# Hybrid attention block: value products in their own PSUM bank, scores in three single banks, sigmoid products on VectorE, and another place for the threshold search

## What is computed

```python
h = _rmsnorm(x, g_in)
proj = h @ w_in            # queries, keys, values, gate paths of A, B, C, and merge gates
y_a = _sliding_window_sink_attention(a_q, a_k, a_v, attn_sinks)
# B: per query, an indexer's scores pick 256 keys, and only these are attended to
score = jnp.einsum('bqhs,bqh->bqs', jax.nn.relu(logits), wb)
_, sel = lax.top_k(score, topk)
y_c = _memory_cross_attention(c_q, m_k, m_v)
ys = jnp.stack([y_a * jax.nn.silu(a_z), y_b * jax.nn.silu(b_z), y_c * jax.nn.silu(c_z)], axis=2)
u = jnp.einsum('bsnc,ncd->bsnd', ys, w_branch)
merged = jnp.sum(jax.nn.sigmoid(gates.reshape(b, s, N_BRANCH, D_MODEL)) * u, axis=2)
return x + merged @ w_out  # then a final RMSNorm
```

## Time and profile before

| what | us |
|---|---|
| median of 3 runs | 3220.39 |
| lowest and highest | 3218.98, 3224.93 |
| the profiled execution, its own time | 3227.78 |
| its span, from first to last instruction | 3225.8 |
| TensorE matmuls busy in it | 2703.2 |
| VectorE busy | 1658.9 |
| ScalarE busy | 1426.6 |
| GpSimd busy | 607.9 |
| mean granted TensorE clock | 0.926 of 2.4 GHz |

### The profile page before, as it was taken

How to read it: one execution, slowest core, us unless ns; L and a number is a source line. 1 busy time by engine, 2 the same in 40 slices (tenths; PEclk the granted TensorE clock), 3 DMA queues, 4 the chain that set the end, 5 groups by cost and what they waited for, 6 DMA issues and landing times.

```text
span 3225.8 us, 37577 instructions
## 1 busy us (share of the span) xinstructions
PE 2703.2 (84%) x13724; PEld 2257.2 (70%) x13724; DVE 1658.9 (51%) x3208; ACT 1426.6 (44%) x2598; POOL 607.9 (19%) x473
## 2 busy tenths in 40 slices
PE   5989896788898987988898987898889969667796
PEld 4777775666687876766787866786667758566685
DVE  4454544332553647323654657732386575666621
ACT  4454543342553624332753535543286455344521
POOL 4435262252111210111111210011101102000020
PEclk9999997989899999989999988998999989888998
DMA  5557283275353340254353340025433505100044
GB/s 167 188 165 254 89 271 91 83 251 169 131 169 119 124 138 1 98 177 134 120 168 119 119 136 7 1 78 185 136 131 123 162 21 192 52 1 1 1 136 158
DMA packets 169701, 392.28 MB, mean 122 GB/s; under 512 B 12848, under 2 KB 95792, under 8 KB 159536
## 3 DMA queue, kind: packets, MB, share of 16 engines
q1 hardware_dynamic: 169520, 389.89, 37.0%
HBM read 301.76 MB, written 88.08 MB: 121 GB/s over the span
## 4 chain that ended last, share of the span: by engine, by line
PE 54%; DVE 19%; ACT 10%; issue 8%; POOL 5%; DMA 3%; SPq 0%; ACTq 0%; DVEq 0%; POOLq 0%
PE PJ L684 39%; PE TR L572 6%; PE PJ L642 3%; DVE prob L1147 3%; DVE ptL L1185 3%; ACT prob L795 2%; ACT ptH L817 2%; POOL pairs L960 2%; ACT squared L774 1%; DVE ranks L1279 1%; DVE above L1226 1%; DMA xs<-in_x 1%; ACT prob L805 1%; DVE zs L1215 1%; PE SC L712 1%
## 5 line engine op out<-in xcount | busy, mean ns | idle before, releaser
L684 PE MATMUL PJ<-hH,pairs 128*128 128x512 f32 (+1 forms) x3584 | 1129.1, 391 | 12.2 <-POOL pairs L960 6.8
L684 PEld LDWEIGHTS PJ<-hH,pairs 128*128 128x128 f32 x3584 | 675.5, 190 | 155.8 <-POOL pairs L960 8.7
L684 PE MATMUL PJ<-hL,pairs 128*128 128x512 f32 (+2 forms) x1792 | 697.5, 389 | 0.0
L572 PE MATMUL TR<-identR,prob 128*128 128x128 f32 x1480 | 260.5, 303 | 206.5 <-ACT prob L795 156.1
L1185 DVE TENSOR_TENSOR ptL<-TR,ptH 128x512 fp32r<-128x512 f32 (+1 forms) x384 | 255.6, 669 | 266.0 <-ACT ptH L817 264.3
L684 PEld LDWEIGHTS PJ<-hL,pairs 128*128 128x128 f32 (+1 forms) x1792 | 340.0, 190 | 67.8
L1226 DVE TENSOR_SCALAR_CACHE_REDUCE above<-score,bits 128x256 uint8<-128x256 f32 (+10 forms) x280 | 348.1, 1243 | 54.3 <-POOL zs L996 45.1
L572 PEld LDWEIGHTS TR<-identR,prob 128*128 128x128 f32 x1480 | 192.0, 155 | 260.9 <-ACT prob L795 175.4
L828 ACT ACTIVATE signs<-score,bits 128x384 bf16<-128x384 f32 (+7 forms) x256 | 334.6, 1307 | 80.4 <-DVE bits L1239 73.1
L817 ACT ACTIVATE ptH<-TR 128x512 fp32r<-128x512 f32 (+1 forms) x384 | 219.2, 580 | 313.0 <-PE TR L572 312.6
L684 PE MATMUL PJ<-ysH,pairs 128*128 128x512 f32 x768 | 250.1, 397 | 26.2 <-ACT sg L883 16.8
(11 more groups left out here) (197 smaller groups left out, 4102.9 us busy)
## 6 DMA issues: line engine op xcount, KB each, us to landing
pairs<-w_split SPq DMA_DIRECT2D x444, 512.0 KB, 4.3
w_split<-pairs SPq DMA_DIRECT2D x74, 1024.0 KB, 4.8
raw<-in_w_in SPq DMA_DIRECT2D x106, 256.0 KB, 5.6
xs<-in_x SPq DMA_DIRECT2D x4, 2048.0 KB, 10.6
rows<-in_x SPq DMA_DIRECT2D x4, 2048.0 KB, 7.9
out<-rows SPq DMA_DIRECT2D x4, 2048.0 KB, 7.5
raw<-in_w_branch SPq DMA_DIRECT2D x24, 256.0 KB, 6.0
memkv<-mem_scratch SPq DMA_DIRECT2D x3, 2048.0 KB, 12.2
```

The lines of the kernel that those rows point to most:

```text
L572: last = nc.tensor.transpose(bank, src, identR[0:k, 0:k].bitcast(F32))
L684: last = nc.tensor.matmul(o, lhs[:, k, :], rhs[:, row, 0:st.n_tok], start=(k == 0 and i == 0 and (up or half == 0)), stop=(k == BC - 1 and ...
```

## The change

1. **Banks.** Value products have a bank PV of their own, one, in place of a share in PJ's two. Scores have three banks of 512 columns in place of two of 1024, so pieces of scores have 512 columns at most (`chunked(it.keys, T)`), and masking and maxima go by such pieces. In A and C the scores of the next item alone are made ahead, after an item's first turn. `ptH` and `ptL` have two buffers each in place of three, so a high part waits until the products of two ticks before are done.
2. **Sigmoid products.** sigmoid(z) is written as (tanh(z / 2) + 1) / 2. ScalarE writes the tanh, and VectorE makes (tanh + 1) times the bank in one pass. The halves are made good where the products are split. The copies into `ub` go, and so do GpSimd's multiplications; GpSimd keeps the additions into `merged`. VectorE makes the low parts of cq and of the memory keys.
3. **The list.** The step `attention` could have units woven between its ticks; `group.woven` is empty, and the units come behind it. Two z units are woven into the index stage. The units of a branch now stand behind the next attention: the first two gates of branch C behind attention C, the rest of branch C and two gates of A behind attention A, the rest of A and two gates of B behind attention B.
4. **The search.** 3 parts after each cq and after each of A's first two z, one in each item of C, two in each turned tile of A, four in each item of A (two in each tick), and what is left before the exact threshold. None stands among gate and up units or the two woven z units.
5. **Buffers.** Keys and values of A's window lie elsewhere, the selection's flags are half-width floats, and its third pass is made in two.

```diff
-PER_UNIT, PER_PAIR, PER_ITEM = (2, 2, 2, 2), ((2, 2, 3), (2, 2, 3), (2, 1, 2), (1, 1, 2)), (0, 0, 0, 1)
+PER_UNIT, PER_C, PER_TURN, PER_A = 3, 1, 2, 4
...
+                for c, size in chunked(it.keys, T):
+                    it.chunks.append((e, c, size, take("s")))
+                    s_freed.append(event("dve_s") if branch == "b" else ("p_exp", n["e"] + len(it.chunks)))
...
-            it.parts = counted(g, PER_ITEM[g]) if branch != "b" else None
+            it.parts = counted(g, {"a": PER_A, "c": PER_C}[branch]) if branch != "b" else None
...
+        group.woven = {}
         steps.append(group)
+        steps.extend(units)
...
-                if st.role == "q" and counting is not None:
-                    select_bits(counting, 1)
+                if counting is not None:
+                    select_bits(counting, PER_TURN)
...
+        st.woven = spread_over(beside, range(-1, len(st.parts) + 1), PRODUCTS // 2)
         steps.append(st)
+        for i in range(4):
+            queries = unit("cq", "w_in", C_Q + i * P, i=i)
+            select_bits(g, PER_UNIT)
+        attention("c", g, branch_units(2, g, 0, 2), queries.used)
+        split_y()
...
         PJ = [ctx.enter_context(nc.psum_tensor(f"PJ{i}", [P, T], F32)) for i in range(2)]
+        PV = ctx.enter_context(nc.psum_tensor("PV", [P, T], F32))
...
-        SC = [ctx.enter_context(nc.psum_tensor(f"SC{i}", [P, 1024], F32)) for i in range(2)]
+        SC = [ctx.enter_context(nc.psum_tensor(f"SC{i}", [P, T], F32)) for i in range(3)]
...
-                if p >= 3:
-                    act.wait_ge(S["pv_done"], p - 2)
+                if p >= 2:
+                    act.wait_ge(S["pv_done"], p - 1)
...
+                elif st.role == "gate":
+                    wait_free(act, x_freed, st.x)
+                    nc.scalar.activation(sg[:, st.x % 2, :], bank, ACT.Tanh, scale=0.5).then_inc(S["act_pj"], 1)
...
+                        gate = sg[:, (st.x + half) % 2, :]
+                        STT(merged[:, st.m + half, :] if st.first else gate, gate, 1.0, PJ[(st.u + half) % 2][:, :],
+                            ALU.add, ALU.mult).then_inc(S["dve_pj"], 1)
...
-                    link(STT(fl, rk, need[:, tt:tt + 1], fl, ALU.is_le, ALU.mult))
+                    link(TS(fl, fl, need[:, tt:tt + 1], None, ALU.is_le))
+                    link(STT(fl, sc, t, fl, ALU.is_ge, ALU.min))
```

720 lines of the change are left out of this document (391 added, 329 removed).

## The result

| | kernel before | changed kernel |
|---|---|---|
| median of 4 runs (lowest to highest), us | 3219.68 (3215.53 to 3224.93) | 3650.63 (3648.13 to 3659.90) |
| span of the profiled execution | 3225.8 | 3650.9 |
| mean granted TensorE clock | 0.926 | 0.879 |

The ratio is 1.134, with a 95% interval of 1.132 to 1.137. The change makes the kernel slower, as predicted, but by 431 us instead of 232, and the range (3345 to 3550) doesn't hold the time.

The account below looks back on a forecast made before the run. TensorE bounds it: its matmuls plus where it waits. Terms 187 + 34 + 33 + 10 + 21 - 30 - 15 - 8 = +232 on 3227.8 give 3460, less 7.4 is 3452 us; range 3345 to 3550.

Parts of the forecast that it names:

- +187 for attention A: Attention A's four stages: two counts per tick lengthen each item's chain, +175, and +12 in groups 0 and 1.
- the 9 to 15 forecast: Attention A, expected sign: TensorE idles there for an item period of 9 to 15 us by group.
- rival (1): Search counts cost their own length and no more: A +147, C +10, turning +12; 3337 us; chance 0.16.
- C and turning: C queries and attention C, +34; turning for A, +33, and A's first gates, +10, from search bits placed there.
- 4 to 17 us later: Attention C, expected sign: its first turn comes this much later in the groups' order, behind the query units' queue.
- the first gates, at +10: A's first gates: 1.5 bits each leave a backlog of 6, 3 and 1 us before the first key tile.
- Index and selection: Index stage with two gate units inside, -30; selection starting sooner after the projections and losing six bare counts, -15.
- The sigmoids' products on VectorE: Projection units: VectorE gains a pass of about 0.7 us, ScalarE loses a copy, both under TensorE's 5.44; 0.
- Attention B, the step that failed: Attention B's four stages: smaller score pieces, two high/low buffers, more pieces in the last tick; +21, bounds -30 and +60.
- +1.0 on most of 16 items: Attention B, groups 1 and 2: more pieces in an item's last tick, +14 and +12.
- The rest: -8: Group 0: GpSimd splits weights and gives up multiplications; -8, bounds 0 to -15.
- Rival (2), the clock: TensorE's clock stays at 1.2 GHz in A and C: +70, 3522 us; sign: periods over 13 us; chance 0.16.

Follow-up runs that it names:

- n1: The changed kernel with one bit of the threshold search in place of 32 and the threshold set to zero; 3409.7 us, ratio 1.060.
- n0: The kernel before with one bit of the threshold search in place of 32 and the threshold set to zero; 3172.6 us, ratio 0.986.
- b3: The kernel before with two waits tightened, as if it had two high/low buffers and one value bank; 3362.2 us, ratio 1.044.
- p1: e3 with the next item's score pieces spread over all ticks but the last (group 3 keeps its last piece there); 3479.0 us, ratio 1.080.
- e3: The changed kernel with a second value bank for every second item and a third high/low buffer in groups 0 to 2; 3541.8 us, ratio 1.100.
- b5: The kernel before with the last score piece of the next item put into the item's last tick in B, groups 0 to 2; 3267.2 us, ratio 1.014.
- e2: The changed kernel with a third high/low buffer in groups 0 to 2, group 3 keeping two; 3581.6 us, ratio 1.112.
- e1: The changed kernel with every second item's value products put into a PJ bank, a second value bank; 3576.0 us, ratio 1.111.
- b2: The kernel before with an item's first value products waiting for VectorE's reading of the previous item's, as with one bank; 3237.4 us, ratio 1.005.
- b1: The kernel before with a high part waiting for the value products of two ticks before, as with two high/low buffers; 3307.7 us, ratio 1.026.

## Why the prediction was wrong, point by point

- **Direction, and the search: right.** The +187 for attention A measured +180. An item of group 3 takes 14.3 us, within the 9 to 15 forecast: its first turn waits 6.9 us for the exponentials, that stand behind the counts, and so does the next item's (TensorE's timeline below). The parts of the term were off against each other. I had 1.4 us for a count (2.8 for two), the runs show 153 / 120 = 1.28, so rival (1) had the better price for the count itself, 1.31. That the sum came out so near is partly luck. And with 1.28 for each count A is still 51 us longer than in the kernel before (n1 against n0), where my period held 187 - (120 x 1.4 - 24.5) = 43 and rival (1) nothing, and C's end to A's start grew by 53 where rival (1) had 12. The 180 counts between gate and up units are 172 in the trace (50, 50, 40 and 32); no term hangs on it.

```profile
2897.74 1.12 PE L626 MATMUL TR<-identR,prob 128*128 128x128 f32 x4 [6.91 <-ACT prob L862]
...
2911.99 1.11 PE L626 MATMUL TR<-identR,prob 128*128 128x128 f32 x4 [7.64 <-ACT prob L862]
```

- **C and turning: right in the sum, not in detail.** +43 for +34, and +53 for +43. Attention C's first turn did not come 4 to 17 us later but -4, -1, +3 and +8 (from the last query unit to the first turn 11.3, 10.4, 15.8 and 21.1 us, where it was 15.5, 11.9, 12.4 and 13.2). The queue at the query units was overestimated, and the items' own periods were underestimated. The +53 lies in the turning itself: from its first turn on TensorE to A's start it takes 62, 55, 61 and 66 us where it took 49, 45, 47 and 48, +55 for the +33 forecast, and the first gates, at +10, cost nothing that shows.
- **Index and selection: right.** -32 for -30; the four stages with their gate units took 18.9, 32.5, 42.3 and 50.6 us, 36.1 in the mean. A's end to B's start -14 for -15.
- **The sigmoids' products on VectorE: right, 0.** Between A's end and B's start of group 1, where units stand almost alone, 529 matmuls took 118.5 us where they had taken 117.5. ScalarE's groups by line have 23 table loads in place of 47, 1283 ns each as in the earlier trace rows, and nothing was gained by it. The Trainium skill (ScalarE: Activation LUTs, What ACT_TABLE_LOAD costs) has a drain of about 1380 ns on each. This trace doesn't agree: the 18 loads at the gates of the kernel before start 0.02 us behind the instruction ahead of them, and the measurement decides.
- **Attention B, the step that failed: +21 for +154.** The prediction looked at the two buffers and wrote that they "take 0.9 back, since a high part now waits for the products that stand behind its own turn". That is a price for one link, once an item. The single value bank was given no price at all: the text of the change said "one", and the sum had no term for it. Neither was traced around: the high part waits for the products, the reading of the bank stands behind the low part of that same high part, and the next item's products wait for the reading. The runs give the ring 99 us in the kernel before (b3), which leaves a net 55. The second mis-sized term is the pieces in the last tick, which I had at +1.0 on most of 16 items: +26 for groups 1 and 2. They measured 59 us there in the changed kernel (p1 against e3) and 42 in the kernel before (b5). In group 3, forecast at -7 for the shorter pieces, the changed kernel is 17 us below b3.
- **The rest: -8 for +41.** "VectorE makes the low parts of cq and of the memory keys" was costed at nothing without asking what it is queued behind; the place of the split behind B wasn't looked at.
- **Rival (2), the clock.** TensorE was busy 211 us in A for matmuls that take 150 without the search (n1), at a granted clock of 0.65 to 0.72 against 0.91. So the clock did fall, but TensorE was waiting anyway: A's sum is 395, not the 390 + 70 of the rival, and the item periods of groups 0 and 1 are 10.7 and 11.5 us (85.2 and 92.4 us over eight items), not over 13.
- **The range** was too narrow above, for it took B's bound (+60) from the price of one link. Had the two limits been followed through one item on paper, as the timeline above does, a ring of b3's size could have been in it.

## What to carry to other kernels

When a change takes away a buffer here and a bank there, don't price each alone: write down who waits for whom through one whole item, and look for a closed ring. Limits of 12 and 50 us can make 99 together. Where you cut it matters: the third buffer gave all that both cuts gave in group 1 (e2), the second bank about half (e1). Nor should the last piece of the next item's work stand in the last tick of this one if it can be made earlier: one tick earlier gave 59 us here. A side computation is free beside a busy engine as long as its chain per unit is shorter than the unit (a bit of up to 4.9 us beside 5.44 was nearly free, 7.3 cost the difference and a little more), and almost all of it shows beside an engine that waits.

## What was unexpected

- The granted clock followed TensorE's waits stage by stage: attention A at 0.65 to 0.72 with counts in it and 0.90 to 0.94 without (n1), with the same 273 matmuls a group. Little of the extra 61 us of busy time can have shown: all that the counts cost in A, 153 us, is no more than their own length (120 x 1.31 = 157). A busy time that grows while the clock falls is no sign of more work. The trace's records have only two levels, 1.0 and 0.5 of 2.4 GHz; 0.68 in group 3 is a mixture of both in time.
- The length of a wait is not its price. In b2 TensorE waits 58 us for the value bank in B, and B is 12 us longer; beside two buffers the same wait costs 49 (b3 against b1), since there something stands behind the products.
